# Two transformer blocks in one kernel: state-space inputs moved between partitions by TensorE products instead of DMAs, and conditioning loads in four buffers instead of two

## The reference, cut to what matters

```python
cond = jax.nn.silu(c)
for i in range(DEPTH):
    mod = cond @ ada_w[i] + ada_b[i]                 # 1024 x 6144, twice
    ...
    h = rms_norm_2(x, norm_mix[i]) * (1.0 + sc_m) + sh_m
    y = dsa_attention(h, ...) if i == 0 else s5_mixer(h, ...)
    x = x + g_m * y
...
def s5_mixer(h, ...):
    bu_re = jnp.einsum('blgc,gpc->blgp', u, bb_re)   # u is h in 64 groups of 16 features
    bu_im = jnp.einsum('blgc,gpc->blgp', u, bb_im)
    _, _, x_re, x_im = lax.associative_scan(_complex_scan_op, (ar, ai, bu_re, bu_im), axis=1)
    y = einsum(x_re, c_re) - einsum(x_im, c_im) + d_skip * u
    g = jax.nn.gelu(y)
    ga, gb = jnp.split(g @ w_glu, 2, axis=-1)
    return ga * jax.nn.sigmoid(gb)
```

## Time and profile before

| | |
|---|---|
| median of 3 runs | 1781.01 us (1780.42 to 1784.26) |
| the profiled execution, its own time | 1783.83 us |
| its span, first to last instruction | 1782.1 us |
| PE busy | 1691.1 us, 95% |
| DVE busy | 797.1 us, 45% |
| ACT busy | 298.2 us, 17% |
| mean granted TensorE clock | 0.975 of 2.4 GHz |
| chain that ended last | PE 88%, DVE 8%, the rest under 1% each or about |

### The profile page before, as it was taken

One profiled execution on the slowest core, in us unless ns is written; L12 is line 12 of the kernel. 1 busy time (PEld: TensorE's weight loads), 2 busy tenths in 40 slices (PEclk: granted clock), 3 DMA queues, 4 the chain that ended last, 5 costly groups with the idle time before them and its releaser, 6 DMA issues.

```text
span 1782.1 us, 21562 instructions
## 1 busy us (share of the span) xinstructions
PE 1691.1 (95%) x8586; PEld 1428.3 (80%) x8586; DVE 797.1 (45%) x1732; ACT 298.2 (17%) x660; POOL 58.8 (3%) x84
## 2 busy tenths in 40 slices
PE   7989989999989999999999999999999778999998
PEld 6648878888878877888888785788888667888887
DVE  6644454341156413644345575456541274343310
ACT  2112210000024102100000322322220011122200
POOL 0000000000000000092000000000000000000000
PEclk9999999999999999999999999999999877999999
DMA  6333448865644563666554232244435302444445
GB/s 222 125 135 119 165 157 306 306 246 186 210 159 146 209 233 136 237 218 243 186 165 154 83 118 95 82 137 152 152 129 166 117 15 72 142 154 152 150 160 177
DMA packets 82900, 290.19 MB, mean 163 GB/s; under 512 B 13296, under 2 KB 13296, under 8 KB 82032
## 3 DMA queue, kind: packets, MB, share of 16 engines
q1 hardware_dynamic: 82800, 288.81, 47.8%
HBM read 286.67 MB, written 1.05 MB: 161 GB/s over the span
## 4 chain that ended last, share of the span: by engine, by line
PE 88%; DVE 8%; issue 1%; DMA 1%; ACT 1%; SPq 1%; DVEq 0%; ACTq 0%
PE acc L381 69%; PE acc L454 5%; PE acc L908 3%; PE acc L436 3%; PE acc L391 1%; PE score L582 1%; PE acc L558 1%; PE turned L593 1%; PE score L538 1%; DVE H L1383 1%; DVE rstd L1319 1%; PE acc L606 1%; SPq L348 1%; DMA ring<-stream 0%; DMA cols<-cols_in 0%
## 5 line engine op out<-in xcount | busy, mean ns | idle before, releaser
L381 PE MATMUL acc<-H,ring 128*128 128x256 f32 x3528 | 777.6, 382 | 21.7 <-DMA ring<-stream 9.9
L381 PEld LDWEIGHTS acc<-H,ring 128*128 128x128 f32 x3528 | 671.5, 191 | 126.0 <-issue 12.2
L381 PE MATMUL acc<-FFN,ring 128*128 128x256 f32 x1408 | 306.5, 381 | 0.0
L381 PEld LDWEIGHTS acc<-FFN,ring 128*128 128x128 f32 x1408 | 268.5, 191 | 37.2 <-issue 0.4
L381 PE MATMUL acc<-big,ring 128*128 128x256 f32 x880 | 192.1, 379 | 0.9 <-PE acc L381 0.9
L381 PEld LDWEIGHTS acc<-big,ring 128*128 128x128 f32 x880 | 166.9, 190 | 24.6 <-issue 2.0
L1538 DVE SCALAR_TENSOR_TENSOR bT<-bT,cond 128x1024 f32<-128x1024 f32 x84 | 109.0, 1298 | 68.1 <-DMA bT<-ada_in 61.0
L1735 DVE SCALAR_TENSOR_TENSOR pair<-acc,cols,pair 128x255 f32<-128x255 f32 x84 | 40.5, 482 | 121.5 <-ACT pair L1077 118.2
L1401 DVE TENSOR_TENSOR X<-acc,X 128x256 f32<-128x256 f32 x48 | 20.4, 425 | 156.1 <-PE acc L381 146.9
L1698 DVE TENSOR_TENSOR FFN<-pair,acc 128x256 f32<-128x256 f32 x42 | 17.7, 421 | 143.0 <-PE acc L381 142.1
L1403 DVE SCALAR_TENSOR_TENSOR X<-acc,mod,X 128x256 f32<-128x256 f32 x24 | 11.6, 484 | 147.9 <-PE acc L381 144.4
(11 more groups left out here) (407 smaller groups left out, 1327.4 us busy)
## 6 DMA issues: line engine op xcount, KB each, us to landing
ring<-stream SPq DMA_DIRECT2D x440, 512.0 KB, 3.3
bT<-ada_in SPq DMA_DIRECT2D x96, 512.0 KB, 4.4
big<-ssm_in SPq DMA_DIRECT2D x2, 1024.0 KB, 5.7
cols<-cols_in SPq DMA_DIRECT2D x1, 1169.5 KB, 7.2
X<-x_in SPq DMA_DIRECT2D x1, 1024.0 KB, 4.8
MEM<-mem_in SPq DMA_DIRECT2D x1, 1024.0 KB, 12.1
FFN<-H SPq DMA_DIRECT2D x32, 32.0 KB, 1.9
y_out<-X SPq DMA_DIRECT2D x1, 1024.0 KB, 3.9
```

What stands on the lines that cost most here:

```text
L381: mm = nc.tensor.matmul(dst, w[:, k * cols_per:(k + 1) * cols_per], r, start=first and n == 0, stop=last and n == len(src) - 1)
```

## The change

**State-space part.** The 32 DMAs are gone. DVE now does one instruction a tile, gain times `rstd` times `X`, into `FFN` tiles 16 to 23, and signals each (`s5_gained`). ACT adds the shift and sets the chunk positions apart into `H` (`shifted(n)`). PE brings the blocks to their partitions with products by pieces of the identity (`select(n)`, 16 products, so 32 PE instructions, on 32 columns of the array each) into the banks `turned` and `stat` in turn, and ACT copies that to `FFN` (`moved(n)`). `driven(n)` waits for `moved(n)` alone. The eight selects and the first four locals are interleaved in PE's program with `driven` 0 and 1. DVE's step works on both parts at once where it can: 512 elements in one instruction for the second product, the scan and the product on the way back, nine instructions in place of twelve. In its first step (n = 0) DVE waits ahead of its last two instructions until ACT has finished all eight `shifted`, since their output goes over `FFN` tiles that these still read.

**Conditioning.** The first 54 loads go to four buffers (two in `K`), load a waiting for load a - 4; the later ones to two. In `up0` none stands behind slots 4 to 7 any more; the 36 are placed behind slots 0 to 3, 8 to 31, and eight later ones. In `od_xb` they stand behind slots 0, 1, 6, 7, and DVE uses them after tiles 2, 3, 6, 7.

```diff
-    ("up0", list(range(28)) + list(range(28, 44, 2))), ("down0", range(0, 24, 4)), ("od_xb", range(0, 8, 2)),
+    ("up0", [0, 1, 2, 3] + list(range(8, 32)) + [32, 34, 36, 38, 40, 41, 42, 43]), ("down0", range(0, 24, 4)),
+    ("od_xb", (0, 1, 6, 7)),
...
+N_WIDE = 54
+ADA_HOME = [a % (4 if a < N_WIDE else 2) for a in range(N_ADA)]
...
-                    if ada >= 2:
-                        sp.wait_ge(ada_used, ada - 1)
+                    if ADA_FREE[ada]:
+                        sp.wait_ge(ada_used, ADA_FREE[ada])
...
+            def select(n):
+                i = S5_ORDER[n]
+                pe.wait_ge(s5_shifted, n + 1)
+                if n >= 2:
+                    pe.wait_ge(s5_moved, n - 1)
+                for jj in range(4):
+                    for j in range(CHUNK):
+                        mm = nc.tensor.matmul(turned[n % 2][32 * j:32 * j + 32, jj * CHUNKS:(jj + 1) * CHUNKS],
+                                              ident[:, 32 * jj:32 * jj + 32],
+                                              H[:, i * S + j * CHUNKS:i * S + (j + 1) * CHUNKS], start=True, stop=True)
+                mm.then_inc(s5_selected, 1)
...
+            def shifted(n):
+                act.wait_ge(s5_gained, n + 1)
+                nc.scalar.activation(at(H, i).rearrange("p (j c) -> p j c", j=CHUNK),
+                                     at(FFN, 16 + i).rearrange("p (c j) -> p j c", j=CHUNK), ACT.Identity,
+                                     bias=mod[:, 48 + i:48 + i + 1]).then_inc(s5_shifted, 1)
...
+            shifted(0)
+            for n in range(1, KD):
+                shifted(n)
+                moved(n - 1)
+            moved(KD - 1)
...
-            scaled(X, KD, rstd[:], lambda k: mod_gain(1, 0, k), H, shift=lambda k: mod_col(1, 0, k), by_chunk=True)
+            for n, i in enumerate(S5_ORDER):
+                v.scalar_tensor_tensor(at(FFN, 16 + i), at(X, i), mod_gain(1, 0, i), rstd[:], ALU.mult, ALU.mult)\
+                    .then_inc(s5_gained, 1)
...
-                own(v.tensor_tensor_scan(w[:, re], d, z[:, re], 0.0, ALU.mult, ALU.add))
-                own(v.tensor_tensor_scan(w[:, im], d, z[:, im], 0.0, ALU.mult, ALU.add))
+                own(v.tensor_tensor_scan(w, d, z, 0.0, ALU.mult, ALU.add))
...
+                if n == 0:
+                    dve.wait_ge(s5_shifted, KD)
...
-                if 2 <= k < 6:
+                if k in (2, 3, 6, 7):
                     ada(1)
```

More of the change, by code:

```diff
@@ L66 @@
 assert N_ADA == 96 and ADA_AFTER == sorted(ADA_AFTER)
+N_WIDE = 54
+ADA_HOME = [a % (4 if a < N_WIDE else 2) for a in range(N_ADA)]
+ADA_TURN = [ADA_HOME[:a].count(ADA_HOME[a]) + 1 for a in range(N_ADA)]
+ADA_FREE = [max((b + 1 for b in range(a) if ADA_HOME[b] == ADA_HOME[a]), default=0) for a in range(N_ADA)]
 PARTS0, _n = {}, 0
@@ L93 @@
 EV_ORDER = (7, 5, 3, 1, 6, 4, 2, 0)
-S5_NORMED = 42
 HEADS = (MLA_H, MEM_H, MEM_H, DSA_H)
@@ L195, in build_program @@
         bT = sb("bT", 2 * STATE_TILES * P)
-        ada_ring = [bT[:, i * SLOT:(i + 1) * SLOT] for i in range(2)]
+        ada_ring = [bT[:, i * SLOT:(i + 1) * SLOT] for i in range(2)] + [K[:, i * SLOT:(i + 1) * SLOT] for i in range(2)]
         ada_acc = bT[:, 2 * SLOT:8 * SLOT]
@@ L242, in build_program @@
         mod_done = sem("mod_done")
-        ada_loaded = [sem(f"ada_loaded{i}") for i in range(2)]
+        ada_loaded = [sem(f"ada_loaded{i}") for i in range(4)]
         ada_used = sem("ada_used")
@@ L270, in build_program @@
         s5_kernels_out = sem("s5_kernels_out")
-        s5_moved = [sem(f"s5_moved{i}") for i in range(2)]
+        s5_gained = sem("s5_gained")
+        s5_shifted = sem("s5_shifted")
+        s5_selected = sem("s5_selected")
+        s5_moved = sem("s5_moved")
         s5_driven = sem("s5_driven")
@@ L340, in _ @@
                     sp.dma_start(V, ssm_in[1]).then_inc(c_in, 16)
[L341 to L350, removed]
             sp.wait_ge(acc_free, 4 + TILE0["down3"] + 8)
@@ L891, in _ @@
             pe.wait_ge(s5_kernels_out, 1)
-            for n in range(4):
-                local(n)
+            select(0)
+            select(1)
+            local(0)
             driven(0)
+            select(2)
             driven(1)
+            select(3)
+            local(1)
+            select(4)
+            select(5)
+            local(2)
+            select(6)
+            select(7)
+            local(3)
             for n in range(KD):
@@ L1332, in inverse_rms, with scaled @@
                 inverse_root(out)
-            def scaled(src, tiles, factor, gain, dst, first=0, to=0, shift=None, by_chunk=False):
+            def scaled(src, tiles, factor, gain, dst, first=0, to=0, shift=None):
                 for lo in reversed(range(0, tiles, 2)):
@@ L1338, in scaled @@
                     rows = factor.unsqueeze(1).broadcast_to([P, m, S])
-                    mid = at(FFN, 8 + lo, m) if by_chunk else at(dst, to + lo, m)
+                    mid = at(dst, to + lo, m)
                     own(v.tensor_tensor(by_tile(mid), by_tile(at(src, first + lo, m)), rows, ALU.mult))
@@ L1530, in ada @@
                     layer, cb, k = a // 48, a // 8 % 6, a % 8
-                    dve.wait_ge(ada_loaded[a % 2], 16 * (a // 2 + 1))
+                    dve.wait_ge(ada_loaded[ADA_HOME[a]], 16 * ADA_TURN[a])
+                    row = ada_ring[ADA_HOME[a]]
                     if a == 48:
@@ L1535, in ada @@
                     if k == 0:
-                        own(v.tensor_scalar(sums, ada_ring[a % 2], cond[:, k:k + 1], None, ALU.mult))
+                        own(v.tensor_scalar(sums, row, cond[:, k:k + 1], None, ALU.mult))
                     else:
-                        own(v.scalar_tensor_tensor(sums, ada_ring[a % 2], cond[:, k:k + 1], sums, ALU.mult, ALU.add))
+                        own(v.scalar_tensor_tensor(sums, row, cond[:, k:k + 1], sums, ALU.mult, ALU.add))
                     dve.sem_inc(ada_used, 1)
@@ L1786, in local_kernels @@
                 own(v.memset(late[:], 0.0))
-                own(v.memset(probs[:, 0:2 * S], 0.0))
+                own(v.memset(probs[:, 0:4 * S].rearrange("p (q c) -> p q c", c=CHUNKS)[:, :, 0:1], 0.0))
                 for g, dst in enumerate((V, late)):
```

46 lines of the change are left out of this document (22 added, 24 removed).

## The result

The changed kernel took 1767.6 us in the median of four runs (1765.0 to 1769.0), the kernel before beside it 1780.7 (1780.2 to 1784.3): a ratio of 0.992, with a 95% interval of 0.990 to 0.994. It is 13.1 us faster, a little more than half of the 23.7 that was forecast. The profiled execution was the lowest of the four, 1765.0 with a span of 1763.2, while the profiled one of before was among the highest of its own (span 1782.1).

What follows compares the result with a forecast made beforehand. PE was taken as the bound, with DVE bounding the state-space steps. `up0` -5.8, `od_xb` -7.4 and the state-space part -10.5 sum to -23.7 us, from the median 1781.01 to 1757.3, given as 1757; range 1750 to 1768.

Steps and rivals of the forecast that it cites:

- One part of the sum: `up0`: the removed stop and its clock loss, less waits of the pairs, would save a net 5.8 us.
- rival (4): Better: clock up early in the state-space part and no waits in the pairs, -29.4 us, 1752; chance 0.13.
- The removed stop: `up0`: PE's 5.2 us stop for a weight load and 3.0 us of clock loss go, 8.2 us saved.
- the last eight loads: `up0`: the last eight conditioning loads have three or more tiles of lead, so cost 0 us.
- the pairs: `up0`: later conditioning loads make PE wait 0.2 us a pair over 12 pairs, 2.4 us lost; bounds 0 and 14.
- the prediction's own sign of being wrong: `up0`: conditioning loads landing after more than 5 us would show the forecast wrong.
- rival (2): Four buffers but no lead: pairs in `up0` wait 1.2 us each, 14 us lost, -12 in all, 1769; chance 0.09.
- rival (3): Slower: pair waits in `up0` grow with landing time, kernel slower from about 6.5 us, 1785 at 6.8; chance 0.03.
- slot 7: `od_xb`: its load lands at about 513.8, wanted at 515.8, so 2 us of cover; a stop there would show error.
- Both branches: State-space part: 8.4 us saved if PE's clock stays low, 13.8 if high from `driven(0)` on.
- The 10.5: State-space part: us saved, taken between 8.4 and 13.8, nearer the low-clock figure.
- Rival (1): Clock stays low through PE's extra state-space work: only 3 us saved there, -16.2 in all, 1765; chance 0.17.

Runs made afterwards that it cites:

- the second set: The unedited changed kernel run again beside the next experiments: 1772.5 us against 1782.4 for the kernel before, ratio 0.994.
- the first trace: Profiled execution of the changed kernel in its first measurement, against the kernel before: 1765.0 us, the lowest of four runs, median 1767.6.
- the second trace: Profiled execution of the unedited changed kernel when run again: the highest of five runs, span 1775.8 us, median 1772.5.
- the filling: 24 unread matmuls on PE during the norm, added to the changed kernel with old `up0` slots: 1755.1 us with DVE's wait for `shifted`, 1753.5 without.

## Why the prediction was right and wrong

**The time** lies inside the range and the direction held, but 1767.6 is 10.6 above the forecast, and 1772.5 in the second set lies above the range's end of 1768. One part of the sum had the wrong sign: `up0` missed by 11.4 us. That the first time stayed inside the range is partly luck, since the state-space part gave 3.8 more than forecast, by the better of its two branches, and the rest of the kernel 2.8 more, in which the change has no part. With the slots as they were, the other terms hold: 29.8 us measured, where rival (4) had 29.4.

**`up0`, the step that failed.** The removed stop was sized right: 161.4 - 153.1 = 8.4 against 8.2. What went wrong is the sentence that the last eight loads "have three or more tiles of lead and cost nothing". It looked at the slots and at PE's tiles, and not at what stands behind the wait in DVE's program. Pair 17's conditioning step had been free because its load was early; once it waits, 9.4 us of `lru_parameters` wait with it. Moving that block ahead of the step removed the stop but for 1.5 us, and moving the slots back removed all of it. It costs 9.0 us, of the 11.4 by which the stage was missed; the pairs make 2.6, and the removed stop gives 0.2 back.

**`up0`, the pairs.** The mechanism was right: each pair's steps wait for a load issued right behind a weight load, and PE stops where the load lands late. But it was three or four stops in an execution and not 0.2 us a pair, and the size was 2.4 us where the executions showed 5.0 and 10.8. The earlier trace rows were a fair sample of landings (median 4.3 forecast, mostly 4.4 to 4.8 measured), but the later ones do the harm, because an early load gives nothing back: of the 24 loads behind slots 8 to 31, three landed after more than 5 us in the first trace (5.1 to 5.6) and seven in the second (5.4 to 6.8). Landings over 5 us in `up0` were the prediction's own sign of being wrong. In the second trace the granted clock around the wait of 2.47 was 0.83 and 0.92 in the two stretches of 7 us from 278 on, where it was 1.00 in the first: at most 1.8 us more. This is rival (2) in part of the runs: 10.8 us is near the 14 that it priced. Its carried-on form, rival (3), was not reached.

**`od_xb`** came out as worked out, 7.35 for 7.4, and slot 7 caused no stop.

**The state-space part.** Both branches were measured: 14.3, 13.4 (60.95, 61.84) with the clock back before or in `driven(0)`, against 13.8 forecast; 8.5 with it low, against 8.4, and the wait 1.88 and 5.78 against 2.0 and 5.9. The step is 6.22 as forecast, and the scan of 512 elements 1.22 against 1.23. Wrong was the choice between the branches. The 10.5 leaned on the low clock, because of the row at 1433 in the earlier trace rows; nine of the ten profiled executions of the new order without the filling had the early rise. In the kernel before, that row lies behind a second stop of 5.6 us, which the new order no longer has. Why the clock came back late in the tenth, no run shows. Rival (1) in its worst form, 3 saved, was not seen.

**The strided read.** `shifted` took 0.75 us in all eight instructions, against 0.47 for the same size with a bias alone. Those of the earlier trace rows read PSUM, though, and `shifted` reads SBUF; an activation of after that reads SBUF without a step, with a factor for each partition, took 0.50 (L1177, 495 ns in the mean of eight). The row of `shifted` (min, median, max in ns):

```profile
L1265 ACT ACTIVATE H<-FFN,mod x8: 747/754/761, 1409.0 to 1422.1; 128x256 f32<-128x256 f32 x8
```

So the trace agrees with the Trainium skill, SBUF — State Buffer, Specifications (TRN2), on cachelines, in that a read which leaves its 16-byte line at each element is slower, by some 0.26 us for 256 elements here; that the step alone does it, no run tested. The prediction's own figure of 0.9 was too much. The other rule is from the Trainium skill, TensorEngine Tiling (Array Packing), Key Properties, on a drain at a change of tiling mode. Between `local`, `select` and `driven` PE's rows follow each other without a bracket of idle time, so a drain cost less here than the 1 us allowed for it.

**Linear scan.** The products cost (0.691 - 0.424) / 256 = 1.04 ns an element more and the scan (1.224 - 0.693) / 256 = 2.07, twice as much. The Trainium skill, DVE: opcode table, instruction layouts, handler registers and perf-mode slots, section Datapath and trigger behaviour, says that the scan runs at half throughput, and the trace agrees. So the wider scan saved only the fixed part of an instruction, 2 x 0.693 - 1.224 = 0.16 us.

**The rest** gave 2.8 us in which the change has no part. It is spread over several stretches (1.0 of it from `glu` on), and whether it is more than scatter stays open.

## What to carry to other kernels

When a load is moved later, look at the whole program of the engine that waits for it: the price is not the lateness but everything queued behind the waiting instruction, here 9.4 us of small work that used to fall into spare time. A load whose consumer gates the bound engine needs lead for its slowest landing, not for its median, and two slots of 3.45 us were enough for 6.7. When a change has two halves, size the halves apart: here one gave all of the gain, and with the slots left as they were the other would have given as much again (1752.6).

## What the runs showed of the hardware

The same program, with the same instructions, had PE's clock at 1.2 GHz for 6.8 us in one execution and for about 20 in another, behind the same idle time of 5.6 us. Why it came back later in one of them, no run shows. PE's work from `select(0)` to the end of `select(5)` took 17.3 us instead of 11.5, and all of these 5.8 us went into the time of the part, since `select(5)` decides when ACT's last `shifted` comes, for which DVE waits. The clock fell at that place in all ten executions in which PE stood idle for 5.6 us, and in neither of the two in which PE was kept at work through the norm.
